# First group's index scores interleaved with the first two chunks of the second in-projection, in a hybrid decoder step

## What is computed

```python
ap = _rmsnorm(hp, norm_mix_pre[layer])
q, k, v, iq, ik, iw, xp = jnp.split(ap @ w_in, cuts, axis=-1)     # q, k, iq, ik are then rotated
# index scores of a query block against all keys, then the 256 best keys
rel = relu(einsum('bnhd,bsd->bnhs', iq, ik_all) * D_IDX ** -0.5)  # 8 index heads
score = einsum('bnh,bnhs->bns', iw * N_IDX_HEADS ** -0.5, rel)
score = where(kpos <= qpos, score, -inf)
_, sel = lax.top_k(score, topk)
```

## Time and profile before

| | us |
|---|---|
| median of 3 runs | 2657.16 (2652.84 to 2662.89) |
| the profiled execution | 2661.24 |
| its span | 2659.4 |
| PE busy | 2541.2 (96%) |
| PE on the chain that ended last | 79% |
| DVE, ACT, POOL busy | 1317.3, 1027.7, 1253.9 |

### The profile page before, as it was taken

How to read it: one execution, slowest core, us unless ns; L and a number is a source line. 1 busy time by engine, 2 the same in 40 slices (tenths; PEclk the granted TensorE clock), 3 DMA queues, 4 the chain that set the end, 5 groups by cost and what they waited for, 6 DMA issues and landing times.

```text
span 2659.4 us, 42175 instructions
## 1 busy us (share of the span) xinstructions
PE 2541.2 (96%) x15118; PEld 2270.7 (85%) x15121; DVE 1317.3 (50%) x1705; ACT 1027.7 (39%) x1534; POOL 1253.9 (47%) x634
## 2 busy tenths in 40 slices
PE   6989869999998999999999999999999999999999
PEld 5779547888886769889999999888889999999999
DVE  4567777889877646554511233621344343220234
ACT  4545654422234645644422222532232435222222
POOL 4545243664665514535544443744543334443442
PEclk8989979999998999999999999999999999999999
DMA  6546012333333142332332232332343221232232
GB/s 154 129 105 154 16 60 64 103 104 93 95 105 113 43 146 68 123 104 87 112 92 70 83 86 72 96 105 85 95 134 119 72 81 43 86 89 75 81 94 68
DMA packets 451034, 246.41 MB, mean 93 GB/s; under 512 B 86668, under 2 KB 439648, under 8 KB 449383
## 3 DMA queue, kind: packets, MB, share of 16 engines
q1 hardware_dynamic: 450927, 244.99, 31.7%
HBM read 221.23 MB, written 23.82 MB: 92 GB/s over the span
## 4 chain that ended last, share of the span: by engine, by line
PE 79%; DVE 4%; ACT 3%; POOL 2%; issue 1%; DMA 1%; SPq 0%; DVEq 0%; POOLq 0%; ACTq 0%
PE psum L884 69%; PE psum L1306 1%; PE psum L1224 1%; PE psum L1328 1%; PE psum L1318 1%; POOL w_lo L2248 1%; DVE probs_t L2844 1%; PE psum L924 1%; PE psum L1049 1%; PE psum L1436 1%; ACT probs_t L1930 1%; PE psum L1075 0%; DVE row_stats L2830 0%; PE psum L1303 0%; DVE z_rows L3129 0%
## 5 line engine op out<-in xcount | busy, mean ns | idle before, releaser
L2248 POOL TENSOR_TENSOR w_lo<-w_raw,w_hi 128x1024 fp32r<-128x1024 f32 (+1 forms) x334 | 858.4, 2570 | 1133.8 <-ACT w_hi L1614 1115.0
L884 PE MATMUL psum<-act_split,w_hi 128*128 128x288 f32 (+1 forms) x5200 | 1049.6, 316 | 5.4 <-POOL w_lo L2248 5.3
L1614 ACT ACTIVATE w_hi<-w_raw 128x1024 fp32r<-128x1024 f32 (+1 forms) x332 | 372.9, 1123 | 1318.1 <-PE psum L884 1260.7
L884 PEld LDWEIGHTS psum<-act_split,w_hi 128*128 128x128 f32 x5200 | 808.2, 189 | 50.0 <-POOL w_lo L2248 5.8
L884 PE MATMUL psum<-act_split,w_lo 128*128 128x288 f32 (+1 forms) x2600 | 647.1, 315 | 0.0
L884 PE MATMUL psum<-hidden_split,w_hi 128*128 128x288 f32 (+1 forms) x2112 | 461.5, 327 | 0.5 <-POOL w_lo L2248 0.5
L884 PEld LDWEIGHTS psum<-act_split,w_lo 128*128 128x128 f32 x2600 | 433.7, 189 | 20.0
L884 PEld LDWEIGHTS psum<-hidden_split,w_hi 128*128 128x128 f32 x2112 | 339.4, 188 | 28.2 <-issue 0.9
L884 PE MATMUL psum<-act_split_first,w_hi 128*128 128x512 f32 x1088 | 340.1, 394 | 0.5 <-POOL w_lo L2248 0.3
L884 PE MATMUL psum<-hidden_split,w_lo 128*128 128x288 f32 (+1 forms) x1056 | 288.0, 327 | 0.0
L2964 DVE TENSOR_TENSOR temps<-psum,temps 128x512 f32<-128x512 f32 (+1 forms) x88 | 63.7, 724 | 358.5 <-PE psum L884 335.5
(11 more groups left out here) (334 smaller groups left out, 2452.9 us busy)
## 6 DMA issues: line engine op xcount, KB each, us to landing
w_raw<-in_w_ffn_gate_up SPq DMA_DIRECT2D x352, 256.0 KB, 3.2
w_raw<-in_w_ffn_down SPq DMA_DIRECT2D x64, 384.0 KB, 3.6
w_raw<-in_w_ffn_down SPq DMA_DIRECT2D x64, 320.0 KB, 4.0
w_raw<-in_w_in_odd SPq DMA_DIRECT2D x64, 256.0 KB, 3.0
w_raw<-in_w_in_even SPq DMA_DIRECT2D x60, 256.0 KB, 3.9
w_raw<-in_w_out_odd SPq DMA_DIRECT2D x32, 256.0 KB, 3.2
x_rows<-in_x_prompt SPq DMA_DIRECT2D x8, 512.0 KB, 6.0
w_raw<-in_w_out_even SPq DMA_DIRECT2D x32, 128.0 KB, 3.0
```

The lines of the kernel that those rows point to most:

```text
L884: mm = pe.matmul(PS[:, 2 * p + b, 0:hi - lo], w[:, p, at], x(k)[:, lo:hi], start=(k == order[0] and w is WH and x is x_hi), stop=(k == ord ...
L1614: act.activation(WH[:, p, 0:n], WR[:, p, 0:n], ACT.Copy).then_inc(S("w_hi"), 1)
L2248: pool.tensor_tensor(WL[:, p, 0:n], WR[:, p, 0:n], WH[:, p, 0:n].bitcast(F32), ALU.subtract).then_inc(S("w_lo"), 1)
```

## The change

1. **Next rows sooner.** The sample rows' transposes go between blocks 5 and 6 after chunk 12; block 7 is transposed inside chunk 13 (before its 7th block). Their squares and sums move with them; the sums' turning goes inside chunk 14 (before its 3rd block) and the spreading ahead of its last block. DVE takes the reciprocal ahead of the last rotation.
2. **Scores among the chunks.** `index(0)` is gone. In the opening of group 1 TensorE does two heads' scores (`first_scores`) ahead of block 0 and after each of blocks 0 to 6 of chunk 0. ACT, DVE and POOL each get a `second_opening` which interleaves relus and high parts (ACT), scaling and weightings (DVE), low parts and the second tile's query parts (POOL). The scores use PSUM banks 6 and 7.
3. **Split index keys and queries of group 0** lie where the rows lay (`x_rows`), no longer in `act_split`.
4. The second chunk's weights are split by ACT in local 14 instead of after `index(0)`.
5. **Top-k rounds:** the two at the start of `in_stage(1)` on DVE are now behind its last rotation (`small(4)` there instead of `small(2)`).

The core of the diff:

```diff
-        IKS = over("idx_keys_split", [P, 2, SEQ], F32R, a_at, 0)
-        IQS = over("idx_queries_split", [P, 2, 8, P], F32R, a_at, 2048)
+        IKS = [over("idx_keys_split0", [P, 2, 512], F32R, h_at, 7552), over("idx_keys_split1", [P, 2, SEQ], F32R, a_at, 0)]
+        IQS = [over("idx_queries_split0", [P, 2, 8, P], F32R, h_at, 8576), over("idx_queries_split1", [P, 2, 8, P], F32R, a_at, 2048)]
...
-        X_AT = {9: (0,), 10: (1, 2), 11: (3, 4), 12: (5, 6), 13: (7,)}
+        X_AT = {9: (0,), 10: (1, 2), 11: (3, 4), 12: (5, "sample", 6)}
...
+            def last_block(k):
+
+                if k == 6:
+                    next_block(NB - 1)
+
+            def next_scale(k):
+
+                if k == 2:
+                    next_sums()
+                if k == 7:
+                    pe.wait_ge(S("rope_out"), 9)
+                    spread(1, 1)
...
+                    if g:
+                        pe.wait_ge(S("ik_lo"), 1)
+                        pe.wait_ge(S("rope_out"), 10)
+                        first_scores(0)
+                        first_scores(1)
                     for k in range(NB + LATE):
                         if k < NB:
                             pe.wait_ge(S("a_lo"), 8 * g + k + 1)
                             block(0, k)
                         if k >= LATE:
+                            if g and k == LATE:
+                                pe.wait_ge(S("nat_a"), 3)
                             block(1, k - LATE)
+                        if g and k < NB - 1:
+                            first_scores(2 * k + 2)
+                            first_scores(2 * k + 3)
...
             in_stage(0)
-            index(0)
-            pe.wait_ge(S("idx_r"), 16)
-            spread(1, 1)
-            pe.wait_ge(S("nat_a"), 3)
             in_stage(1)
...
                         if local == 13:
-                            next_sample()
-                if g == 0:
-                    root(1, 1)
+                            root(1, 1)
+                            act.wait_ge(S("xt_ps"), 17)
+                            act.activation(IKS[0][:, 0, :], IKT[:, 0:512], ACT.Copy).then_inc(S("ik_hi"), 1)
+                            index_queries(0, 0)
...
+            def second_opening():
+
+                act.wait_ge(S("w_used"), phase("in", 0).c0 + 15)
+                split(1, 0, 1)
+                for k in range(NB):
+                    relus(0, k // 4, IDX_T[0][k // 4], 2 * k % 8)
+                    relus(0, k // 4, IDX_T[0][k // 4], 2 * k % 8 + 1)
+                    if k < NB - 1:
+                        split(1, k + 1, 1)
...
+                index_queries_lo(0, 0)
+                lo_part(ph.next, 0, ph.slot(14))
+                for n in range(NB):
+                    split(1, n, 1)
+                    if n == 1:
+                        pool.wait_ge(S("a_lo"), 10)
+                        index_queries_lo(0, 1)
...
+            def second_opening():
+
+                dve.wait_ge(S("n_b"), 2)
+                dve.wait_ge(S("xt_cp"), 17)
+                dve.wait_ge(S("rope_out"), 10)
+                split(1, 1, Y, G_MIX_PRE, 0, (0, 1))
+                for k in range(NB):
+                    u, t = k // 4, IDX_T[0][k // 4]
+                    weigh(0, u, t, 2 * k % 8)
+                    weigh(0, u, t, 2 * k % 8 + 1)
+                    if k + 2 < NB:
+                        split(1, 1, Y, G_MIX_PRE, 0, (k + 2,))
+                    if k % 4 == 3:
+                        weighed(u, t)
...
                     dve.tensor_copy(XPE[:, :, 0:BUF], XPE[:, :, 512:512 + BUF]).then_inc(S("halo"), 1)
-                    small(2)
...
+                        if g == 0 and local == 13:
+                            next_block(NB - 1)
+                            next_sum(NB - 1)
+                            sample_sum()
+                            inverse(1, 1)
                         rotate(local)
...
                 if g:
-                    small(2)
+                    small(4)
```

More of the change, by code:

```diff
@@ L1209, in in_stage, with scores, first_scores, index @@
                 rows_of(SQ[:, off, 0:T[g]], P, 2 * off, g, IDENT)
[L1211 to L1216, removed]
-                    for h in range(8):
[L1218 to L1230, removed]
+            def scores(g, u, t, h):
+                n = P * (t + 1)
+                k = 1 if n <= 512 else 2
+                w = n // k
+                pe.wait_ge(S("iq_lo"), 2 * u + h // 4 + 1)
+                wait(pe, S("idx_r"), 8 * u + h - 1)
+                for part in range(2):
+                    for b in range(k):
+                        mm = pe.matmul(PS[:, idx_bank(g, h) + b, 0:w], IQS[g][:, u % 2, h, :], IKS[g][:, part, b * w:b * w + w],
+                                       start=part == 0, stop=part == 1)
+                mm.then_inc(S("idx_mm"), 1)
+            def first_scores(j):
+                scores(0, j // 8, IDX_T[0][j // 8], j % 8)
+            def index():
+                pe.wait_ge(S("ik_lo"), 2)
+                pe.wait_ge(S("rope_out"), 20)
+                for u, t in zip(IDX_U[1], IDX_T[1]):
+                    for h in range(8):
+                        scores(1, u, t, h)
+                        index_sample(8 * (u - 2) + h)
+                mix(DB - 1)
             def turn(b):
@@ L1545, in _ @@
             in_stage(0)
[L1546 to L1549 removed]
             in_stage(1)
[L1551 removed]
+            index()
             attend(0)
@@ L2162, in _ @@
             in_stage(0)
-            index(0)
-            for n in range(NB):
-                split(1, n, 1)
+            second_opening()
             in_stage(1)
-            index(1)
+            index()
             def out_aside(c):
@@ new lines, in second_opening, with index @@
+            def second_opening():
+                ph = phase("in", 0)
+                pool.wait_ge(S("rope_t2"), 10)
+                pool.wait_ge(S("w_lo"), ph.c0 + 16)
+                index_queries_lo(0, 0)
[5 more added lines that the diff above has]
+                        index_queries_lo(0, 1)
+            def index():
+                ph = phase("in", 1)
+                pool.wait_ge(S("rope_t2"), 20)
+                pool.wait_ge(S("w_lo"), ph.c0 + 16)
+                for u in IDX_U[1]:
+                    index_queries_lo(1, u)
+                queries(0, 0)
+                queries(0, 1)
@@ L2500, in scaled, with split @@
                 return PS[:, 5:7, P:P + HALF[1][1]]
-            def split(a, g, src, base, layer):
-                for n in range(NB):
+            def split(a, g, src, base, layer, blocks=range(NB)):
+                for n in blocks:
                     wait(dve, S("a_lo"), 8 * a + n - 1)
@@ L3202, in _ @@
             in_stage(0)
-            index(0)
-            next_split()
+            second_opening()
             in_stage(1)
-            index(1)
+            index()
             def out_aside(c):
```

182 lines of the change are left out of this document (94 added, 88 removed).

## The result

The changed kernel takes 2662.50 us (median of 20 runs, 2655.90 to 2668.82) against 2658.42 us for the kernel before (20 runs, 2652.63 to 2662.92): ratio 1.0017, 95% interval 1.0010 to 1.0024, so 4 us slower. It is 0.3 us from the forecast of 2662.8, and that closeness is luck: the forecast added 5.6 us to a median of three runs, 2657.16, which twenty runs put at 2658.42.

What follows compares the result with a forecast made beforehand. It took TensorE, 79% of the chain that ended last, as the bound. The queue's 2.9 us and the late rounds' 2.7 made 5.6, added to the median 2657.16 for 2662.8 us; 8 in 10 range 2650 to 2671.

Steps and rivals of the forecast that it cites:

- Part 1: Chunks 12 to 14: earlier transposes and sums bring the opening's first product to 143.5 from 160.98, 17.5 us sooner.
- Part 2: Opening with 16 heads' scores: 28 us instead of 16, ending at 171.5 instead of 176.9, so 5.4 us left.
- my four values: Last weighting's end: 168.3 upper clock, 164.3 without collisions, 169.4 lower clock until 160, 174 lower throughout.
- The collisions: In the opening, DVE's weightings and POOL's low parts take turns at one SBUF port pair, costing about 4 us.
- Part 3: SyncE's queue: page gathers wait for the last weighting, delaying weight loads, turning 5.4 us won into 2.9 lost.
- 2.9 us later: Chunk 4's load issued at 180.2 instead of 177.31, passed on whole to chunk 11, starting at 245.0.
- Part 4: Two top-k rounds moved behind DVE's last rotation, where it has no gap, delay the key split by 2.7 us.
- The sum: Whole kernel: 2.9 us from the queue plus 2.7 from late rounds, 5.6 us added, giving 2662.8 us.
- B: Queue has room: TensorE keeps its 5.4 us and pays 2.7, 2654.5 us or down to 2648; chance 0.21.
- C: Opening stays at 1.2 GHz, TensorE sets the pace at 4.4 us per block: 2667 to 2675 us; chance 0.14.
- Its last part: TensorE's stand before chunk 3 brings the lower clock again, up to 5 us more.
- D: All 17.5 us kept, scores costing nothing beside the products and nothing later bound: 2640 to 2643 us; chance 0.03.

Runs made afterwards that it cites:

- after2: The changed kernel, unaltered, profiled and timed once more beside another version: ratio 1.0014 to the kernel before.
- a_rounds: Changed kernel with the two top-k rounds back at the start of the second in-projection: ratio 1.0011 to the kernel before.
- a_psum: Changed kernel with group 0's relus written back to PSUM, so weightings read one operand there: ratio 1.0001 to the kernel before.
- b_gate: Kernel before, with SyncE's first page gather also waiting until DVE has scaled all 8 blocks of group 1's rows: ratio 0.9999.
- b_both: Kernel before with the first gather waiting for DVE's 8 scalings and the two top-k rounds late, no scores moved: ratio 1.0025.
- b_rounds: Kernel before with only the two top-k rounds moved behind the second in-projection's last rotation: ratio 1.0006.
- b_order: Kernel before with only the page gathers reordered, 8 non-overlapping pages first, the weightings' wait behind chunk 4's load: ratio 1.0003.
- a_order: Changed kernel with 8 non-overlapping pages gathered first and the wait for the weightings behind chunk 4's load: ratio 0.9993 to the kernel before.
- a_best: Changed kernel with gathers reordered and the two top-k rounds back at the start: 2654.30 against 2657.91 us for the kernel before.
- a_bp: Changed kernel with gathers reordered, top-k rounds at the start and relus in PSUM: 2654.60 against 2657.91 us for the kernel before.
- a_bp2: Repeat of the changed kernel with gathers reordered, rounds at the start, relus in PSUM: 2650.49 against 2658.23 us for the kernel before.

## Why the prediction was right, and where it was not

**Part 1, rows and sums sooner: right.** The first product came at 144.54, for which I had 143.5 and a range of 142 to 145. The other condition in that part came true as well, in half of the executions: "If the 2 us of standing bring the lower clock, 1 to 3 us less." In the second kind the lower clock came in the middle of chunk 14, cost 1.6 us, and put the first product at 145.5 to 146.3. It was not in the sum.

**Part 2, the opening: right in its pace, a little long.** The last weighting ended at 168.69; my four values were 164.3 to 174, the chosen one 169.5. The opening ended 6.1 us sooner instead of 5.4 (5.1 in after2), and took 26 us instead of 28. The collisions were priced at about 4 us of the path; taken away, they gave 3.1. TensorE had the lower clock until about 150.7, not 160 (my estimate from the window of 150 to 152, which shows 0.82; the next one shows 1.00).

**Part 3, the queue: the mechanism is right, its size was not.** The step "2.9 us later" passed the whole delay of chunk 4's load on to chunk 11. Measured, the load left 2.07 us later (1.5 against the rotation, 2.8 in after2), and chunk 11's weights were 0.1 and 1.4 us later against the rotation. The lost 1.4 lie in one place: from the issue of chunk 5's load to that of chunk 6's there were 11.9 us before (183.35 to 195.23) and 10.5 after (185.42 to 195.92). In this stretch the queue stands behind the 2304 KB copy of `Y` to DRAM. The kernel before, to be set beside the changed kernel's rows above:

```profile
183.35 4.40 SPq L536 DMA_DIRECT2D w_raw<-in_w_in_even  x2
189.72 5.29 SPq L601 DMA_DIRECT2D idx_key_pages<-in_cache_idx_k  x3
195.23 1.01 SPq L536 DMA_DIRECT2D w_raw<-in_w_in_even  x2
```

I had written that the queue "has no waits to give back from 177 to 244"; it has no waits on other engines, but an issue can itself be held up: the two loads right behind the copy took 4.40 us to issue instead of 1.01, in both kernels, and the three gathers behind them 5.29 us before and 3.94 after. Why these shrank I have not shown. All 13 executions fall on two values: 10.5 us where the queue ran without a pause from its first gather to chunk 4's load (after, after2, a_rounds, a_psum, b_gate, b_both), 11.9 where it had stood for 11 us or more ahead of that load (before, b_rounds, b_order, a_order, a_best, a_bp, a_bp2).

**Part 4, the rounds: right.** From the end of chunk 11's low part to the key split there were 34.8 us before (34.8 to 35.1 in every version with two rounds at the start), and 37.5 to 37.8 in every version with late rounds; that is the forecast's 2.7. Behind the last rotation stand eight rounds instead of six; the prediction's last section says six for the changed kernel, and its sum used the difference of two, which is right.

**The sum** was 2.9 + 2.7 = 5.6 on the profiled execution; measured at the key split, 2.9 and 4.1 in two executions, and 4.1 us in the median. The part that was too large by 1.5 to 2.8 us was the queue's. The base it was added to, a median of three runs, was 1.3 us too low, and that brought the forecast back to the measured time.

**The rivals.** B (the queue has room) is excluded by b_gate, a_order and b_order together. C (the lower clock through the opening) did not come: 1.00 from 152. Its last part did: behind the stand before chunk 3 the clock was 0.50 from 182 to 184. That cost nothing at chunk 11, which waits for weights: from the issue of chunk 6's load to the start of chunk 11 there are 46.9 us in both kernels. D was never near (the 19 us of DVE's work named there are 18.0 by part 3's bound; the step is the same).

## What to carry to other kernels

Before work is moved, look up who else waits for it: here a DMA queue's wait for the last step of the moved work had 11.7 us of slack in the old place and none in the new one, and it held weights that had nothing to do with it. If a shared queue waits because of memory that two tiles share, see whether the pieces that don't overlap can go first. And when DVE's work is put beside POOL's, try an operand in PSUM for DVE if one is at hand; here it brought the last weighting 3.1 us forward.

## What the runs showed of the hardware that I had not expected

- Operations of DVE with one tile of SBUF as input and SBUF as output were held by POOL too: the first weighting of a tile took 1.29 us instead of 0.42, the reversed copy of the scores 1.61 instead of 0.36. The same weighting from PSUM, in a_psum, took 0.62 while POOL subtracted. So a PSUM operand is slower where nothing is in the way, and isn't held.

```profile
143.41 1.29 DVE L2807 TENSOR_SCALAR scores_tile<-relu_short,idx_weights 128x384 f32<-128x384 f32 x1 [4.52 <-ACT relu_short L1858]
...
157.16 1.61 DVE L2822 TENSOR_SCALAR scores<-scores_tile 128x384 f32<-128x384 f32 x1
```

```profile
144.47 0.62 DVE L2809 TENSOR_SCALAR scores_tile<-psum,idx_weights 128x384 f32<-128x384 f32 x1 [4.64 <-ACT psum L1861]
```

- The same kernel can start the opening 1.6 us later in another execution (21.0 and 22.6 us behind the rotation, in four and four executions; in the two kernels that were profiled twice, both kinds came up). TensorE waits for the sums inside chunk 14. In the first kind its clock was 1.00 behind that wait, in the second it fell to 0.50 there. In three of the four executions of the first kind the clock had been low ahead of that wait instead, where the wait shrank from 2.0 to 0.5 us and the low clock cost nothing.
